# Delta rule on one core: the chunk inverse closed by halves, and four queues ordered from lengths

## What is computed

```python
decay_mask = exp(where(lower, diff, -inf))
m = where(strict, einsum('bhnck,bhnsk->bhncs', k_beta, k) * decay_mask, 0.0)
t = triangular_solve(eye + m, eye, left_side=True, lower=True, unit_diagonal=True)
u = t @ v_beta
w = t @ (k_beta * exp(gc)[..., None])
attn = einsum('bhnck,bhnsk->bhncs', q, k) * decay_mask

def step(S, xs):
    v_new = u_n - w_n @ S
    o = qd_n @ S + attn_n @ v_new
    S = S * gl_n[..., None, None] + swapaxes(kd_n, -1, -2) @ v_new
    return S, o
```

## Time and profile before

| | us |
|---|---|
| median of 3 runs | 3112.83 (3112.27 to 3114.64) |
| the profiled execution | 3110.53 |
| its span | 3108.7 |
| TensorE busy, weight loads busy | 3053.0, 2813.1 |
| VectorE, ScalarE, POOL busy | 1929.3, 1237.5, 663.4 |
| instructions | 54979 |
| mean granted clock of TensorE | 0.994 |

### The profile page before, as it was taken

How to read it: one execution, slowest core, us unless ns; L and a number is a source line. 1 busy time by engine, 2 the same in 40 slices (tenths; PEclk the granted TensorE clock), 3 DMA queues, 4 the chain that set the end, 5 groups by cost and what they waited for, 6 DMA issues and landing times. The chain is left out here.

```text
span 3108.7 us, 54979 instructions
## 1 busy us (share of the span) xinstructions
PE 3053.0 (98%) x21809; PEld 2813.1 (90%) x21809; DVE 1929.3 (62%) x3550; ACT 1237.5 (40%) x1949; POOL 663.4 (21%) x549
## 2 busy tenths in 40 slices
PE   8998999999999999999999999999999998999999
PEld 8976789999999999999999999998888788778887
DVE  7345499988888768888875323354355366464243
ACT  4235323457777533333334312232234354243232
POOL 0010206863333324433320101101000121201011
PEclk9999999999999999999999999999999899999999
DMA  4210225699999999999982322322222000223231
GB/s 157 82 41 1 95 75 158 196 324 339 343 338 340 355 321 345 357 356 360 355 279 81 106 78 89 96 73 91 99 75 81 23 3 10 88 84 112 82 101 69
DMA packets 160168, 517.34 MB, mean 166 GB/s; under 512 B 18928, under 2 KB 51824, under 8 KB 156656
## 3 DMA queue, kind: packets, MB, share of 16 engines
q1 hardware_dynamic: 75632, 279.93, 26.8%
q0 software_dynamic: 44032, 159.40, 14.7%
q10 hardware_dynamic: 40320, 75.52, 6.6%
HBM read 462.35 MB, written 52.43 MB: 166 GB/s over the span
## 5 line engine op out<-in xcount | busy, mean ns | idle before, releaser
L185 DVE TENSOR_TENSOR w_lo<-ring,w_hi 128x1024 fp32r<-128x1024 f32 (+2 forms) x157 | 205.8, 1311 | 546.7 <-ACT w_hi L179 546.7
L179 ACT ACTIVATE w_hi<-ring 128x1024 fp32r<-128x1024 f32 (+2 forms) x170 | 190.0, 1118 | 433.4 <-PE ps L245 359.8
L245 PE MATMUL ps<-f_hn_hi,w_hi 128*128 128x264 f32 (+1 forms) x1056 | 279.3, 319 | 0.8 <-DVE w_lo L185 0.6
L245 PE MATMUL ps<-f_hn_lo,w_hi 128*128 128x264 f32 (+1 forms) x1056 | 278.6, 318 | 0.0
L245 PE MATMUL ps<-f_hn_hi,w_lo 128*128 128x264 f32 (+1 forms) x1056 | 278.5, 318 | 0.0
L486 ACT ACTIVATE w_hi<-ring 128x1024 fp32r<-128x1024 f32 x170 | 180.1, 1059 | 225.1 <-PE ps L543 222.1
L490 DVE TENSOR_TENSOR w_lo<-ring,w_hi 128x1024 fp32r<-128x1024 f32 x144 | 176.2, 1224 | 111.1 <-ACT w_hi L486 90.2
L543 PE MATMUL ps<-units_hi,w_hi 128*128 128x384 f32 x680 | 227.8, 335 | 3.6 <-DVE units_lo L868 3.6
L514 PE MATMUL ps<-hn_hi,w_hi 128*128 128x384 f32 x680 | 231.3, 340 | 0.0
L543 PE MATMUL ps<-units_lo,w_hi 128*128 128x384 f32 x680 | 227.7, 335 | 0.0
L543 PE MATMUL ps<-units_hi,w_lo 128*128 128x384 f32 x680 | 227.6, 335 | 0.0
(11 more groups left out here) (520 smaller groups left out, 8010.5 us busy)
## 6 DMA issues: line engine op xcount, KB each, us to landing
ring<-in_w_uv SPq DMA_DIRECT2D x256, 512.0 KB
ring<-in_f_up SPq DMA_DIRECT2D x88, 512.0 KB
expert_units<-scratch ACTq DMA_DIRECT2D x128, 192.0 KB
gate_table<-peer ACTq DMA_DIRECT2D x24, 1024.0 KB
peer<-gate_table POOLq DMA_DIRECT2D x64, 384.0 KB
peer<-expert_units ACTq DMA_DIRECT2D x128, 192.0 KB
ring<-in_w_in SPq DMA_DIRECT2D x29, 512.0 KB
ring<-in_w_late SPq DMA_DIRECT2D x25, 512.0 KB
```

What stands on the lines that cost most here:

```text
L179: self.nc.scalar.activation(self.h[:, self.slot(k), 0:self.cols], e.ring[:, self.ring(k), 0:self.cols], ACT.Copy).then_inc(e.hi_done, 1)
L185: self.nc.vector.tensor_tensor(self.l[:, self.slot(k), 0:self.cols], e.ring[:, self.ring(k), 0:self.cols], self.h[:, self.slot(k), 0:self. ...
L245: mm = nc.tensor.matmul(e.ps[:, bank + hf, 0:tokens.width], lhsT[:, wt.slot(k), col], rhs(part, c)[:, cut], start=(c == 0 and j == 0), sto ...
```

## The change

Three things are changed, all within `phase_delta` and its tables.

First, the end of the inverse. "z5", "fw", "fwe", "zte", "f2", "f2e", "v4", "v4e" and "trf" leave the chunks of 128. "z5a" now copies all four inverted blocks to the small tile `b.c`. "g1" transposes them (32x32 products with the identity) and multiplies within each pair of blocks; "g2" completes the two 64x64 inverses and one transposed; "za" and "zb" (VectorE and ScalarE) put the transposed blocks into et, "zd" and "g2e" the corners of the halves; "g3" and "g4" join the halves with two 64x64 products per head in all, with k S in "g3".

Second, the order. `plan` takes a table of lengths in ns for each step (`LENGTH`, `SHORT`, `FIRST`) and a hand-over of 45 ns (`SIGNAL`), and builds all four queues by putting next, each time, the step that can start first. `FLOWS` has no starts any more. "unit" is no member of a group now: POOL does it once the groups ahead of "tr1" are done, counts a semaphore `dl_units` of its own, and only "p4" waits for it.

Third, identity products. `keep_warm` is gone from the region; instead TensorE gets one identity product (`DUMMY` = 224 ns) for each 224 ns of the wait that the planner foresees ahead of some steps of the chunks of 128, into PSUM places that are free there. That makes 21 in all.

```diff
-FLOWS = [(0, 0, 8), (0, 1, 3), (1, 0, 0), (1, 1, 6)]
+FLOWS = [(0, 0), (0, 1), (1, 0), (1, 1)]
+DUMMY = 224
...
-    GROUPS = [("in",), ("args", "save"), ("exps",), ("x1", "eb"), ("tr1", "hold", "unit"), ("tre",), ("p2", "trf", "kd"),
-              ("p2e",), ("p4",), ("p4e", "z2"), ("p8",), ("p8e", "z3"), ("p16",), ("p16e", "z4"), ("z5p",), ("z5", "z5a"),
-              ("fw",), ("fwe", "zte"), ("f2",), ("f2e", "v1e"), ("v4",), ("v4e",), ("vn",), ("vne",), ("o",), ("oe",)]
+    GROUPS = [("in",), ("args", "save"), ("exps",), ("x1", "eb"), ("tr1", "hold"), ("tre",), ("p2", "kd"),
+              ("p2e",), ("p4",), ("p4e", "z2"), ("p8",), ("p8e", "z3"), ("p16",), ("p16e", "z4"), ("z5p",), ("z5a",),
+              ("g1",), ("g1e",), ("g2", "za", "zb"), ("g2e", "zd"), ("g3",), ("g3e", "v1e"), ("g4",), ("g4e",), ("vn",),
+              ("vne",), ("o",), ("oe",)]
...
+    LENGTH = {"in": 710, "tr1": 380, "p2": 455, "p4": 620, "p8": 620, "p16": 455, "z5p": 490, "g1": 380, "g2": 300,
...
+    SIGNAL = 45
...
+        start, ready, i, name, c = min(starts, key=lambda x: x[:3])
+        f, engine = flows[i], flows[i].engine(name)
+        if engine == "PE":
+            idle[f, name, c] = start - free["PE"]
+        end[i, name, c] = start + f.length(name, c)
+        free[engine] = end[i, name, c] - (65 if engine == "PE" else 10)
+        orders[engine].append((f, name, c))
...
-            for step, (f, name, n) in enumerate(turns(flows, "PE")):
-                if step == 2:
-                    keep_warm(nc, e, 0, 10)
-                elif 2 < step < 7:
-                    keep_warm(nc, e, 0, 3)
+            def dummies(f, name, n):
+
+                at = {"in": 1, "g3": 1, "vn": 1, "tr1": 3, "p4": 3, "o": 3}
+                if n and name == "p2" and not f.makes(n):
+                    at["p2"] = 3
+                if n and name in at:
+                    for _ in range(int(idle[f, name, n] // DUMMY)):
+                        M(place(f, at[name], P, P)[:, 0], c["ident"], c["ident"])
...
                 elif name == "p4" and n:
+                    pe.wait_ge(units, unit_at[f, n])
...
-                    if n:
-                        prod(A, U[1], zz)
-                        prod(B, zz, U[1])
                     for h in range(2):
                         mm = TR(C[:, h], zz[:, h], ident)
-                elif name == "f2":
-                    prod(A, U[1], U[0])
-                    prod(C, U[0], zt)
+                elif name == "g1":
+                    tiles(0, (held(2), unit))
+                    for h in range(2):
+                        for i, j in f.pairs():
+                            mm = M(tiny(f, 2)[rows(j), h], U[0][rows(i), h, rows(j)], c3[rows(i), h, 2])
+                elif name == "g2":
+                    for h in range(2):
+                        for i, j in f.pairs():
+                            M(tiny(f, 2)[rows(i), h], c3[rows(j), h, 1], c3[rows(j), h, 0])
+                        j = f.pairs()[0][1]
+                        mm = M(tiny(f, 2)[rows(j), h], c3[rows(j), h, 0], c3[rows(j), h, 1])
+                elif name == "g3":
+                    for h in range(2):
+                        M(A[early, h, 0:P // 2], D[late, h, early], zt[late, h, late])
                     mm = prod(wide, k, b.S)
-                elif name == "v4":
-                    mm = prod(C, V[0], zt)
+                elif name == "g4":
+                    for h in range(2):
+                        mm = M(C[early, h, 0:P // 2], zz[early, h, early], b.u[early, 1, h, 0:P // 2])
...
+                elif name == "zb":
                     for i in (0, 1):
-                        ins = A_(corner(b.zz, i), tiny(f, 2)[i * SUB:(i + 1) * SUB], ACT.Copy)
+                        ins = A_(corner(b.et, i), b.c[rows(i), :, 0], ACT.Copy)
+                elif name == "g2e":
+                    for i, j in f.pairs():
+                        ins = A_(b.et[rows(i), :, rows(j)], tiny(f, 2)[rows(i)], ACT.Copy)
...
-                elif name == "z5":
+                elif name == "za":
                     for i in (2, 3):
-                        ins = V_.tensor_copy(corner(b.zz, i), tiny(f, 2)[i * SUB:(i + 1) * SUB])
+                        ins = V_.tensor_copy(corner(b.et, i), b.c[rows(i), :, 0])
+                elif name == "zd":
+                    i, j = f.pairs()[0]
+                    V_.tensor_copy(corner(b.zz, i), b.c[rows(i), :, 2])
+                    V_.tensor_copy(corner(b.zz, j), b.c[rows(j), :, 2])
+                    ins = V_.tensor_copy(b.zz[rows(j), :, rows(i)], tiny(f, 2)[rows(j)])
...
                 elif name == "v1e":
-                    TT(zt, zt, C, ALU.add)
...
-                elif name == "v4e":
-                    ins = TT(zt, zt, C, ALU.add)
```

More of the change, by code:

```diff
@@ L2616 @@
             ("oe",)]
[L2617 to L2621 removed]
+    ON = {"PE": ("in", "tr1", "p2", "p4", "p8", "p16", "z4p", "z5p", "fw", "g1", "g2", "g3", "g4", "vn", "o"),
+          "ACT": ("save", "exps", "eb", "tre", "p2e", "p4e", "p8e", "p16e", "z5a", "g1e", "zb", "g2e", "g3e", "g4e",
+                  "vne")}
```

128 lines of the change are left out of this document (92 added, 36 removed).

## The result

The changed kernel takes 3119.53 us, the median of 13 runs (3110.57 to 3128.66); the kernel before takes 3107.34 in as many (3099.84 to 3117.30). The ratio is 1.0031 with a 95% interval of 1.0017 to 1.0046: it is slower by about 0.3%, where 3090.3 us and a gain were predicted. The profiled execution took 3113.57 us.

A forecast was written before the change was run, and what follows sets the result against it. TensorE was taken to bound phase_delta. Load terms -39.3 + 4.9 + 7.1 + 4.8 = -22.5 us, gaps unchanged at 27.3, took the 3112.8 us median to 3090.3 us (region 152); range 3074 to 3108.

The forecast's parts named there:

- 124.7 us of load: TensorE's weight loads in phase_delta after the change: 147.2 us less 22.5, bounds -33.3 to -15.4.
- the pace of small products: g1 and g2 add 288 products of 32x32, 576 records at 8.5 ns apiece: +4.9 us of load.
- the term for the gaps: TensorE's gaps in phase_delta kept at 27.3 us, shorter chains set against a longer low-clock stretch.
- half the full pace: g3 and g4 add 128 records of 64x64, taken at half of 0.111 us apiece: +7.1 us of load.
- the 0.20 us for going over: TensorE's extra time for going from full to small tiles, 0.31 us where 0.11 is the pace.
- the 9.5 us: Gain lost if 576 small records cost 14.4 us, by the skill's 25 ns between matmul starts; not taken.
- changes of shape: TensorE goes over to a smaller or another small shape 84 times instead of 60: 24 x 0.20 = +4.8 us.
- Some 10 us longer: A low-clock stretch at the region's start again, some 10 us longer without the 22 wide products: +3.8 us.
- The rival of the low clock: Clock stays low at g3 to vn; gain gone at 0.30 of work low, 3132.8 us at half; chance 0.11.
- the rival of the growing gaps: Latency takes over in phase_delta: loads fill 0.77, region 162 us, total 3100.3 us; chance 0.22.
- The reasons for fewer gaps: Unit off the chain and a shorter inverse end: 1.7 us a chunk, some 7 us along each chain.
- Nothing: Cost of the 21 identity products if their foreseen waits are there; otherwise 0.22 us each, 4.7 us in all.

The follow-up runs named there:

- the alternating order: The changed kernel with a planner rule: after a small TensorE step another small one only if no other shape can start within 0.9 us; ratio to before 0.9952.
- The kernel with the alternating order and none: The alternating order with its 66 identity products left out, the rest as it is; ratio to before 0.9991, region 166.5 us.
- The old inverse in that order: The old inverse (fw, f2, v4) in the alternating order, with 7 identity products; ratio to before 0.9981, region 169.4 us.
- the kernel with small products twice: The kernel before with the small products of p4 and p8 in chunks of 128 issued twice; region 202.3 us against 177.1, one run.

## Why the prediction was wrong

The sum was 124.7 us of load and 27.3 us of gaps, a region of 152. 143.1 and 42.0 came, 185.1. Two steps of it failed: the pace of small products, taken as 8.5 ns a record for any number of them, and the term for the gaps, kept at 27.3 us. By estimate the first accounts, with the clock behind it, for some 20 us of the 33 between 152 and 185 (what the alternating order gave back), the second for some 13, which stay even in that order. Beside this the base of 3112.8 us, from 3 runs, was 5.5 us above the median of 13.

*The load.* The count held, at the clock it was worked out for. 124.7 us were predicted with 21 identity products. The kernel with the alternating order and none has 122.6 us, with 19 us at half clock; with 21 products more (4.7 us) that is 127. The old inverse in that order has 144.7 with 7 of them, 143.1 without, so the new one takes 20.5 us out where 22.5 were predicted. The small terms can be read too, weight loads of the change at full clock:

```profile
2520.87 0.30 PEld L2893 LDWEIGHTS ps<-delta 128*128 128x128 f32 x2
2521.29 0.30 PEld L2880 LDWEIGHTS ps<-delta 64*64 64x64 f32 x4
```

Four loads of 64x64 take 0.30 us, one takes 0.13: (0.30 - 0.13)/3 = 0.057 us apiece, where half the full pace, 0.055, was taken, an estimate that held. The first of them begins 0.31 us after the last full one (2520.98), the 0.20 us for going over as read in the earlier trace rows. In the changed kernel load is still 143.1 us, since 78 us of the region ran at half clock.

*The pace of small products.* This step failed first. "48 such loads take 0.51 us, 8.5 ns apiece" was right for a run of 48 and was taken for any number. A run longer than the instructions at hand goes on at 30 ns a record, and what counts is how many stand close together: 128 small records pass in 1.1 us and a line comes in 3.9. The sum had no term for a standstill. The prediction set aside the rule of the Trainium skill (TensorE: Matmul & The Clock Gate, "Wait — 56ns, not 53.3ns?") of some 25 ns between starts. In the 48 loads the trace still disagrees with it. Over several us the pace comes out near that figure for another reason, the supply of instructions. That is chance, and with the 9.5 us that it would have added the forecast would still have been 3099.8 us, 19.7 below what came.

*The orders.* They are fixed in the kernel, and the prediction went through them for changes of shape only, though it says of them that "small steps of several chains often stand together". Five runs of over 64 small products stand there, 170 the longest, against 40 before. The four chains start at once, so the two forward and the two backward ones reach their small steps together; in the old turns the forward ones were 5 turns apart and the backward ones 6. This was the thing to see, and the planner cannot see it: its table has a length for a step, and no price for two small steps behind each other.

*The clock.* "Some 10 us longer" was said, and it is 61 us longer. The rival of the low clock had the gain gone at 0.30 of the work at half clock, and its price was about right: by its figures an all-low region would be 152 + 97.7 = 250 us, so 78 us of it are 0.31 of the work and take back the gain. The prediction gave this rival 0.11, and put its place at g3 to vn, where wide work goes out. The place is the run of small products from p4 to g2 and the standstill behind it. The argument against it, that a slow TensorE fills its own gaps, failed because gaps at half clock were again for want of instructions (at 2583.9 and 2588.0 us) and because going over to small tiles costs more then:

```profile
2579.04 0.93 PEld L2774 LDWEIGHTS ps<-const_tab 128*128 128x128 f32 x4
...
2580.19 0.73 PEld L2800 LDWEIGHTS ps<-delta 32*32 32x32 f32 x48 [0.22 <-issue]
```

The last of the four full loads began at 2579.63, the small ones at 2580.19: 0.56 us, where 0.31 is the figure at full clock.

*The gaps.* 27.3 us were kept and 42.0 came, 20.1 of them ahead of the 32x32 products with no releaser. The step failed without that, too. In the alternating order without identity products, where no standstill is left, the gaps are 43.9 us beside 122.6 of load. The 66 identity products turn this into 29.7 and 135.1: they stand in the gaps and don't shorten the chains. The old inverse in that order has gaps of 24.7 us with 7 of them (1.6 us), 26.3 without. So the new inverse took 20.5 us out of the load, and 17.6 of it came back as gaps: the region without identity products is 166.5 us, with the old inverse 169.4. Most of the growth is waiting for VectorE and ScalarE, 26 us where it was 10 (idle times over 0.15 us). These are one profile each. This is the rival of the growing gaps, which the prediction gave 0.22: it put the region at 162 us, and the alternating orders have 164.9 to 166.5. The reasons for fewer gaps were true as far as they go (ScalarE waits 3.4 us behind hold in the change where it waited 8.7) and too small.

*Identity products.* "Nothing" was right for the change: without them the region is 0.9 us shorter in one profile. In the alternating order they are worth some 12 us by the ratios.

How much of the 20 us between the change and the alternating order is standstill and how much half clock stays open. The 17.5 us of standstills and what some 70 us of half clock cost overlap, and no run took one away and left the other whole. The steps that the prediction got wrong are shown by the runs; this split is not.

## What to carry to other kernels

Ahead of a change that turns wide TensorE products into many small ones, count how many small ones stand in a row in the final order and set that against the supply of instructions: here some 128 records with their loads in 4 us, so spread them between wide steps of other chains. Don't keep the gaps of an engine as a fixed term when its own work is cut: here 17.6 of 20.5 us taken out of TensorE's load came back as gaps, most of them waits for other engines. A planner that orders queues from the lengths of steps needs a rule for what a sequence costs, or it will save a microsecond of waiting and pay for a standstill and the clock behind it. When a busy engine is idle for no releaser, look at the instruction queue in the DMA view. And before a profile is taken for its kernel, compare its time and mean clock with the median of the runs.

## What the runs showed of the hardware

- TensorE stands still 1.0 to 2.5 us, at either clock, when small products use up its instructions: 256 instructions (128 loads, 128 matmuls) in 3.9 us. In all ten standstills of the change and all six of the kernel with small products twice, a 16 KB transfer of the instruction queue had begun 2.2 to 3.0 us before TensorE went on.
- The granted clock fell behind idle time of TensorE: 25 of 31 falls in the middle of the region come in or at most 2.6 us behind one of over 1.0 us, 17 of them for want of instructions and 8 in waits for ScalarE, while 13 such idle times had no fall behind them.
- It was back after 3.4 us where only wide products followed (three times, in the kernel with small products twice) and after 6.9 to 23.9 us in the change.
- Going over from full to small tiles takes 0.56 us from start to start at half clock and 0.31 us at full clock. A small record takes 13 ns at half clock in the change (48 loads in 0.73 us), 19 ns in the earlier trace rows (64 in 1.34 us), against 8.5 ns at full clock.
- 64x64 float32 records follow each other at 0.057 us at full clock.
